# Attention probabilities split into fp16 halves before they are turned, and turned by DMA transposes

## What is computed

```python
def combine_by_denominator(outs, lses):
    w = jax.nn.softmax(jnp.stack(lses, axis=0), axis=0)
    return jnp.einsum('pbth,pbthe->bthe', w, jnp.stack(outs, axis=0))

def dilated_attention_prompt(q, k, v):
    outs, lses = [], []
    for window, dil in DILATIONS:          # (128, 1), (512, 4), (2048, 16)
        o, l = _banded_dilated(q, k, v, window // dil, dil)
        outs.append(o)
        lses.append(l)
    return combine_by_denominator(outs, lses).astype(q.dtype)
```

## Time and profile before

| | us |
|---|---|
| median of 3 runs | 1707.12 |
| lowest and highest run | 1706.36, 1707.31 |
| span of the profiled execution | 1704.6 |
| busy in it: TensorE | 1547.2 |
| VectorE | 847.6 |
| ScalarE | 457.3 |
| GpSimd | 207.6 |

### The profile page before, as it was taken

The page is one execution under the profiler, slowest core; times in us unless marked ns, Lnnn a source line. Parts: engine busy times, 40 slices in busy tenths (PEclk is TensorE's granted clock), DMA queues, the critical chain, the costliest instruction groups (busy, mean ns, idle before and its releaser), DMA issues. The chain is left out here.

```text
span 1704.6 us, 26185 instructions
## 1 busy us (share of the span) xinstructions
PE 1547.2 (91%) x9324; PEld 878.3 (52%) x9324; DVE 847.6 (50%) x1814; ACT 457.3 (27%) x742; POOL 207.6 (12%) x132
## 2 busy tenths in 40 slices
PE   1699999799999987489799899999999999999996
PEld 1355555456565653134344466546664466645652
DVE  6566766436465576566511245413553145512557
ACT  2321221135344451022311144302441034400310
POOL 3310001010101012422100011100110001100125
PEclk9999999798899998689899999999999999999998
DMA  7001101120202025631100422201221022201002
GB/s 217 25 26 51 35 16 38 37 63 3 61 10 59 26 76 154 215 118 49 53 10 1 128 60 79 58 0 37 74 74 37 15 59 74 74 0 38 13 2 103
DMA packets 107311, 96.62 MB, mean 57 GB/s; under 512 B 6407, under 2 KB 91223, under 8 KB 106983
## 3 DMA queue, kind: packets, MB, share of 16 engines
q1 hardware_dynamic: 107247, 95.77, 18.8%
HBM read 85.78 MB, written 10.15 MB: 56 GB/s over the span
## 5 line engine op out<-in xcount | busy, mean ns | idle before, releaser
L1529 PE MATMUL PS<-all_HT,all_WS 128*128 128x344 f16 x3168 | 465.0, 310 | 4.8 <-POOLq L74 4.8
L1529 PEld LDWEIGHTS PS<-all_HT,all_WS 128*128 128x128 f16 x3168 | 310.5, 98 | 159.7 <-issue 6.6
L1539 PE MATMUL PS<-all_WS,ffn_HG 128*128 128x512 f16 (+1 forms) x792 | 237.7, 379 | 3.9 <-POOL ffn_HG L1624 1.9
L442 PE MATMUL PS<-all_WS,all_HT 128*128 (+3 forms) x864 | 194.5, 382 | 3.8 <-POOLq L74 3.8
L1598 ACT ACTIVATE ffn_C<-PS,all_CW,all_CWS 128x1032 f32<-128x1032 f32 x44 | 53.0, 1205 | 379.8 <-PE PS L1529 379.8
L740 PE MATMUL PS<-all_WS,all_HT 128*128 (+3 forms) x864 | 148.4, 329 | 5.5 <-POOLq L74 3.4
L1539 PE MATMUL PS<-ffn_WD,ffn_HG 128*128 128x512 f16 (+1 forms) x396 | 150.1, 379 | 0.0
L1624 POOL TENSOR_TENSOR ffn_HG<-ffn_PRD,ffn_HG 128x1032 f32 (+1 forms) x22 | 47.2, 2146 | 766.4 <-ACT ffn_HG L1610 766.4
L442 PEld LDWEIGHTS PS<-all_WS,all_HT 128*128 128x128 f16 (+1 forms) x864 | 83.7, 97 | 101.4 <-POOLq L74 3.9
L1539 PEld LDWEIGHTS PS<-all_WS,ffn_HG 128*128 (+2 forms) x792 | 76.5, 97 | 101.1 <-issue 8.2
L740 PEld LDWEIGHTS PS<-all_WS,all_HT 128*128 128x128 f16 (+1 forms) x864 | 82.8, 97 | 60.8 <-issue 8.5
(11 more groups left out here) (198 smaller groups left out, 1862.0 us busy)
## 6 DMA issues: line engine op xcount, KB each, us to landing
ffn_SU<-in_w_up SPq DMA_DIRECT2D x42, 512.0 KB, 5.0
ffn_SD<-in_w_down SPq DMA_DIRECT2D x22, 512.0 KB, 3.4
all_STG<-in_w_in SPq DMA_DIRECT2D x32, 256.0 KB, 3.2
all_STG<-in_w_in SPq DMA_DIRECT2D x32, 192.0 KB, 2.7
samples_KC<-in_cache_k_win SPq DMA_DIRECT2D x24, 256.0 KB, 3.8
all_HRES<-in_x_prompt SPq DMA_DIRECT2D x8, 512.0 KB, 5.4
out<-attention_QKV SPq DMA_DIRECT2D x8, 512.0 KB
all_STG<-in_w_out SPq DMA_DIRECT2D x8, 512.0 KB, 3.8
```

The costliest lines, as they stand in the source:

```text
L442: mm = nc.tensor.matmul(Z(s)[:n], HT[:, a, k, s * P:s * P + n], WS[:, slot, b, k, :], start=(k == 0 and (a, b) == (0, 0)), stop=(k == KD - ...
L1529: mm = nc.tensor.matmul(U(x)[:, third], UW[:, u, a, k, x * P:(x + 1) * P], HT[:, b, k, third * T3:(third + 1) * T3], start=(k == 0 and (a, ...
L1539: mm = nc.tensor.matmul(DB[u][:rows, half], HG[:, a, l, ds(t * P, rows)], WD[b][:, l, half * 512:(half + 1) * 512], start=(l == 0 and (a, ...
```

## The change

ScalarE makes the high half straight from PR in SBUF one call after the exp (into the new buffer P16), GpSimd makes the low half as PR minus the high half, and SP issues two DMA transposes for each unit, SBUF to SBUF, that write the turned blocks into PRT. TensorE no longer turns the probabilities, and VectorE no longer makes the low half. PRT now has six slots (even units in PRTL, eight blocks wide; odd ones in PRTS, four wide), and the products of unit n stand five calls behind its scores instead of four (LAG). VectorE's maximum of unit n waits for the low half of unit n - 3. SP's program is written out for the four pairs instead of looped; the transposes of a pair stand behind its output stores and ahead of the next pair's weight loads, and the last two of the eight `w_out` loads stand behind the transposes of units 4 and 8 of the last pair. Each slot of PRT has a semaphore of its own.

```diff
-            PRT = sb(st, "PRT", [P, 3, 2, NT, P], F16)
+            P16 = sb(st, "P16", [P, 3, 2, SEQ], F16)
+            PRTL = sb(st, "PRTL", [P, 3, 2, NT, P], F16)
+            PRTS = sb(st, "PRTS", [P, 3, 2, NT // 2, P], F16)
...
-            PT = (PS[:, 3:5], PS[:, 5:6])
+
+            def PRT(m):
+
+                return (PRTL if m % 2 == 0 else PRTS)[:, m // 2 % 3]
+
+            LAG = 5
...
+            p_turned = sems("p_turned0 p_turned1 p_turned2 p_turned3 p_turned4 p_turned5")
+
+            def turns(p, m):
+
+                used = (NQ + 5 - m % 6) // 6
+                return 32 * used * p + 32 * (m // 6 + 1)
...
                 @block.sync
...
+                        for n in range(NQ):
+                            q = Q_ORDER[n][1]
+                            w = (q + 1) * P
+                            sp.wait_ge(o_ready, BASE + NQ * p + (n - 5 if n >= 6 else (-3, -2, -1, 0, -4, -4)[n]))
+                            for a, ready in ((0, p_hi), (1, p_lo)):
+                                sp.wait_ge(ready, BASE + NQ * p + n + 1)
+                                sp.dma_start_transpose(PRT(n)[:, a, 0:q + 1], P16[:, n % 3, a, 0:w]).then_inc(p_turned[n % 6], 16)
+                            if last and n in (4, 8):
+                                load_out(5 + n // 4)
...
                 @block.gpsimd
...
+                        for n in range(NQ):
+                            w = (Q_ORDER[n][1] + 1) * P
+                            pool.wait_ge(p_hi, BASE + NQ * p + n + 1)
+                            if n >= 3:
+                                pool.wait_ge(p_turned[(n - 3) % 6], BASE + turns(p, n - 3))
...
+                            nc.gpsimd.tensor_tensor(P16[:, n % 3, 1, 0:w], PR[:, n % 3, 0:w], P16[:, n % 3, 0, 0:w],
+                                                    ALU.subtract).then_inc(p_lo, 1)
...
                 @block.tensor
...
-                        m = n - 2
-                        if 0 <= m < NQ:
-                            pe.wait_ge(exp_ready, BASE + NQ * p + m + 1)
...
-                            for kb in range(q + 1):
-                                mm = nc.tensor.transpose(PT[m % 2][:, kb // 4, (kb % 4) * P:(kb % 4 + 1) * P],
-                                                         PR[:, m % 3, kb * P:(kb + 1) * P], IDENT[:])
-                            mm.then_inc(p_turned, 1)
-                        m = n - 4
+                        m = n - LAG
                         if 0 <= m < NQ:
                             h, q = Q_ORDER[m]
-                            pe.wait_ge(prt_low, BASE + NQ * p + m + 1)
+                            pe.wait_ge(p_turned[m % 6], BASE + turns(p, m))
...
                 @block.scalar
...
-                            nc.scalar.activation(PRT[:, m % 3, 0, 0:q + 1],
-                                                 PT[m % 2].rearrange("p b (k n) -> p (b k) n", k=4)[:, 0:q + 1], ACT.Copy).then_inc(prt_ready, 1)
...
+                        m = n - 1
+                        if 0 <= m < NQ:
+                            w = (Q_ORDER[m][1] + 1) * P
+                            act.wait_ge(exp_ready, BASE + NQ * p + m + 1)
+                            if m >= 3:
+                                act.wait_ge(p_turned[(m - 3) % 6], BASE + turns(p, m - 3))
...
+                            nc.scalar.activation(P16[:, m % 3, 0, 0:w], PR[:, m % 3, 0:w], ACT.Copy).then_inc(p_hi, 1)
...
                 @block.vector
...
-                        m = n - 3
-                        if 0 <= m < NQ:
-                            q = Q_ORDER[m][1]
-                            dve.wait_ge(prt_ready, BASE + NQ * p + m + 1)
-                            nc.vector.tensor_tensor(PRT[:, m % 3, 1, 0:q + 1],
-                                                    PT[m % 2].rearrange("p b (k n) -> p (b k) n", k=4)[:, 0:q + 1],
-                                                    PRT[:, m % 3, 0, 0:q + 1], ALU.subtract).then_inc(prt_low, 1)
...
-                            dve.wait_ge(p_turned, BASE + NQ * p + n - 2)
+                            dve.wait_ge(p_lo, BASE + NQ * p + n - 2)
...
-    nc = bacc.Bacc("TRN2", target_bir_lowering=False, num_devices=1)
+    nc = bacc.Bacc("TRN2", target_bir_lowering=False, num_devices=1, dynamic_dma_scratch_size=1024)
```

More of the change, by code:

```diff
@@ L656, in body, with load_out @@
                                              w_in_v[:, 2 * c + k, 4:7, p + 1, :]).then_inc(w_in_s[c % 2], 16)
-                        for k in range(KD if last else 0):
+                        def load_out(k):
                             sp.wait_ge(w_free, BASE + 4 * p + k + 1)
                             sp.dma_start(STG[:, k % 2], w_out[0, k * P:(k + 1) * P].rearrange("p (c n) -> p c n", c=2)).then_inc(w_in_s[k % 2], 16)
+                        for k in range(6 if last else 0):
+                            load_out(k)
                         sp.wait_ge(rotated, BASE + 18 * p + 18)
@@ L668, in body @@
                                      QKV[:NB, NT].rearrange("b (j n) -> b j n", j=3)).then_inc(out_st, 16)
-                    steps(body)(sp)
+                        for n in range(NQ):
[7 more added lines that the diff above has]
+                                load_out(5 + n // 4)
+                    for p in range(HP):
+                        body(sp, p, p == HP - 1)
                     sp.wait_ge(out_st, BASE + 80 * HP)
@@ L683, in body @@
                         nc.gpsimd.tensor_tensor(V16[:, 1], QKV[:, 0:NT, 256:384], V16[:, 0], ALU.subtract).then_inc(v_lo, 1)
+                        for n in range(NQ):
[3 more added lines that the diff above has]
+                                pool.wait_ge(p_turned[(n - 3) % 6], BASE + turns(p, n - 3))
+                            elif not isinstance(p, int) or p > 0:
+                                pool.wait_ge(p_turned[(NQ + n - 3) % 6], BASE + turns(p - 1, NQ + n - 3))
+                            pool.sem_inc(pool_go, 1)
+                            nc.gpsimd.tensor_tensor(P16[:, n % 3, 1, 0:w], PR[:, n % 3, 0:w], P16[:, n % 3, 0, 0:w],
+                                                    ALU.subtract).then_inc(p_lo, 1)
                     steps(body)(pool)
@@ L750, in body @@
                                 mm.then_inc(z_turned, 1)
-                            if kind != "first" and s < 4:
+                            if kind != "first" and s < LAG:
                                 attend(NQ + s, p - 1)
@@ L754, in body @@
                                 pe.wait_ge(att_ready, BASE + NQ * p)
+                                pe.wait_ge(mlo, BASE + p - 1)
                                 for t in range(NT):
@@ L791, in attend @@
                                                  bias=NMX[:, n % 3:n % 3 + 1], accum_out=SUM[:, n % 8:n % 8 + 1]).then_inc(exp_ready, 1)
+                        m = n - 1
[4 more added lines that the diff above has]
+                                act.wait_ge(p_turned[(m - 3) % 6], BASE + turns(p, m - 3))
+                            elif not isinstance(p, int) or p > 0:
+                                act.wait_ge(p_turned[(NQ + m - 3) % 6], BASE + turns(p - 1, NQ + m - 3))
+                            nc.scalar.activation(P16[:, m % 3, 0, 0:w], PR[:, m % 3, 0:w], ACT.Copy).then_inc(p_hi, 1)
                     def body(act, p, kind):
@@ L799, in body @@
                         for s in range(NT + 2):
-                            if kind != "first" and s < 2:
+                            if kind != "first" and s < 1:
                                 attend(NQ + s, p - 1, False)
@@ L860, in attend @@
                                                     ALU.mult, ALU.add).then_inc(neg_ready, 1)
-                        m = n - 5
+                        m = n - LAG - 1
                         if 0 <= m < NQ:
@@ L874, in body @@
                         for s in range(NT + 1):
-                            if kind != "first" and s < 5:
+                            if kind != "first" and s < LAG + 1:
                                 attend(NQ + s, p - 1, False)
```

15 lines of the change are left out of this document (3 added, 12 removed).

## The result

The changed kernel takes **1740.88 us** (median of 4 runs, 1738.58 to 1743.91), the kernel before 1706.91 in the runs beside it: ratio **1.020, 95% interval 1.0183 to 1.0217**. The forecast was 1732 (1710 to 1755), and slower.

What follows compares the result with a forecast made beforehand. Attend phases were bound by TensorE at half clock, then by VectorE; after the change, by half-clock TensorE. Phases +9, projections +12, tail +4 give +25: 1704.6 + 25 + 2.5 = 1732 us, range 1710 to 1755.

Steps and rivals of the forecast that it cites:

- my two readings: DMA moving price of one 128x128 block: 0.22 us taken from packet costs, 0.12 us from the output stores' rate.
- C: Rival for the attend phases: reading and writing each cost a packet, 0.45 us a block, 1822 us in all; chance 0.20.
- D: Rival for the DMA transposes: blocks go one after another at 1.07 us each, about 2140 us in all; chance 0.13.
- Rival A: Attend phases: cheap blocks and issues, clock comes back, ScalarE paces at 28.8 us a phase; 1689 us in all; chance 0.32.
- three times 36.8: Attend phases before the change: the first three taken at 36.8 us each, the last at 33.2.
- my own 38.1: Attend phase after the change: 35.1 us of TensorE work at half clock plus 3 us idle, 38.1 us.
- not the bound: Path through SP's transposes in the attend phase: unit 10 lands at 34.2 us, so TensorE bounds instead.
- A unit comes every 2.14 us: SP's transposes in the attend phase: 32 issues of 1.07 us take 34.2 us a pair.
- 9.0 us after the first score: Start of the attend phase: when the first low half is ready, after exps, copy and GpSimd's subtraction.
- 8 us at half clock lose 4 each: Start of three projections: each begins at half clock for 8 us and loses 4, +12 us together.
- The late weight loads: Next pair's weight loads, queued behind SP's transposes: land 2.7 us after issue, put at no cost.
- some of it in place of TensorE's turn: Tail after the last pair: open chain of copy, subtraction, issue and landing, partly replacing TensorE's turn; +4 us.

Runs made afterwards that it cites:

- e11: e10 plus ten more unused identity turns on TensorE ahead of the first pair's first score; 1692.34 us, 0.993 of the kernel before.
- e12: The kernel before the change, with ten unused identity turns on TensorE ahead of the first pair's first score; 1705.55 us, ratio 0.9994.
- e5: The changed kernel with one matmul pass of three in the attention's scores and products; 1730.3 us, ratio 1.0124.
- e7: e1 with products seven calls behind the scores instead of five and four buffers for the halves instead of three; 1723.84 us, ratio 1.0093.
- e9: e7 with four buffers for the fp32 probabilities, sixteen sums, and the last call's copy ahead of this call's exp; 1715.26 us, ratio 1.0045.
- e1: The changed kernel with both halves of a unit turned by one transpose, 16 issues a pair instead of 32; 1738.98 us, ratio 1.0192.
- e8: e7 with the unused identity turns of e2 on TensorE; 1729.69 us, ratio 1.0128.
- e10: e9 with the unused identity turns of e2 on TensorE; 1704.01 us, ratio 0.9982.
- e4: The changed kernel with the subtraction on VectorE, two calls behind, in place of GpSimd; 1775.57 us, ratio 1.0396.
- e6: e1 with one matmul pass of three in the attention's scores and products; 1712.02 us, ratio 1.0026.
- e2: The changed kernel with as many unused identity turns behind the scores as TensorE lost; 1751.71 us, ratio 1.0271.

## Why the prediction was right, and where not

**Right in sign and on the clock, in part on what holds the phase.** L844 and its 48.0 us are gone from VectorE, whose busy time fell by 36.6 us, and it was worth nothing: TensorE's clock stayed at 0.51 for the whole phase. Its work there is 34.5 us against 35.1 forecast. ScalarE's copy came out at 672 ns (forecast 673). GpSimd's subtraction took 20.8 us a pair (19). The block cost 0.19 us: from 385 to 412 us the transposes made 12779 packets in 69.6% of 16 x 27 us, 23.5 ns each, and a block is 128 of them over 16 engines. That is between my two readings (0.22 taken, 0.12 the low end), and C and D fall. Rival A falls as made, but e11 shows that its full clock can be had in a loosened version with added turns, whose phases of 29.2 to 33.4 us (44 blocks of products) stand against A's 28.8 (55).

The total is nearer than its terms: the phases came out 12.8 us and the tail 4.4 over the forecast, the projections 7.4 under it. That these cancel in part is luck.

**The phases, +21.8 for +9.** Two steps failed. The first is "three times 36.8": the third phase of before takes 33.2 us, and I had carried the first one's row over to it. With the phases as they are (37.4 + 36.6 + 33.2) my own 38.1 would have given +12. Nor is 33.2 a fixed length: the same code takes 35.9 us in the third phase of e12.

The other 9.8 us come from the path through the issues, which I had called "not the bound". I priced an issue at 1.07 us by the scratch store; it costs 1.24. "A unit comes every 2.14 us" and lands, for unit 10, "at 34.2": unit 0 is issued at 380.45 and unit 10 at 408.45, 2.8 us a unit, with waits between. Its second transpose is issued 1.3 us later and with the median landing of 2.7 is there at about 412.5, 39 us after the first score; the phase takes 40.8. I had compared SP with TensorE as if the longer of the two would be the phase, and had put TensorE at half clock first. e5 turns that round: the issues hold a phase of 38.5 us with TensorE 38% busy, and TensorE's other two passes add 2.3. That e7, at 37.9 us, comes near my 38.1 is a coincidence of lengths: its phase has 72 x 0.346 + 44 x 0.186 = 33.1 us of work and some 5 of waits, where my sum had 35.1 and 3, and e9 brings it to 36.5.

Two smaller sums are off and change nothing: the terms of "9.0 us after the first score" add up to 9.3, and C with 0.53 us a block gives about 1858, not 1865.

**The projections, +4.6 for +12.** "8 us at half clock lose 4 each" was too much. The clock was back in under 6 us: 0.65 on average from 414.35 to 420.30, which loses 5.95 x 0.35 = 2.1 us. I had taken the time of the last phase of before, where TensorE waits between scores. The late weight loads cost nothing I can find: TensorE was busy 41.7 of 43.95 us.

**The tail, +8.4 for +4.** I added the new chain once, "some of it in place of TensorE's turn". Behind the last score the products of several units are still open, and each waits for its own transpose and at half clock (TensorE's timeline of the changed kernel):

```profile
672.53 1.14 PE L747 MATMUL PS<-attention_V,attention_PRTL 128*128 128x64 f16 x18 [1.43 <-DMA attention_PRTL<-attention_P]
676.02 0.50 PE L747 MATMUL PS<-attention_V,attention_PRTS 128*128 128x64 f16 x6 [2.35 <-DMA attention_PRTS<-attention_P]
678.58 0.98 PE L747 MATMUL PS<-attention_V,attention_PRTL 128*128 128x64 f16 x15 [2.06 <-DMA attention_PRTL<-attention_P]
680.93 0.34 PE L747 MATMUL PS<-attention_V,attention_PRTS 128*128 128x64 f16 x3 [1.37 <-DMA attention_PRTS<-attention_P]
```

The steps of 2.4 to 3.5 us between them are SP's rhythm again, where each unit's product takes 0.3 to 1.1 us. With half the issues (e1) the tail is 15.1 us in place of 19.4.

**The rule and the rows.** The Trainium skill, VectorE: DVE Perf Modes, section "The three transpose paths", has 1309 ns for one 128x128 block through the DMA. That is of the size of one issue here (1.24 us), but issues of one to eight blocks cost the same and a block in flow costs 0.19 us, so taking 144 blocks one after another by it would be wrong; the traces decide. The Trainium skill, DMA: Bandwidth & Descriptors, section "Latency and other measured facts", has 261 GB/s for transposes with a middle dimension that is not contiguous, an estimated 0.13 us a block, closer than the other and still below the 0.19 measured.

**What stays open.** Why TensorE stayed at half clock through a phase in which it was always busy (e8, e10) is open. In e10 and e11 the second phase has the clock at 0.90 and takes 4 us more than the third; no run says why. e10's executions range from 1702.0 to 1712.4 us and e11's from 1688.1 to 1703.7, mostly with lower mean clocks in the longer ones, so how long the clock stays up isn't fixed. Whether GpSimd's long subtraction cost the changed kernel anything wasn't separated, since e4 brought a wait of its own. Nor was the gain of e7 split between its buffers and its lag.

## What to carry to other kernels

Work taken off TensorE can take its clock with it: here 75 matmuls fewer in the first phase left it busy as long, at 0.51 in place of 0.77. Price the stretch at half clock first, and only then ask which other engine is next. A DMA transpose has a price per instruction on the queue that issues it (1.24 us here), so put as many blocks as the data allow into one, and give the path behind it buffers and lag for the 2.3 to 4.9 us that it took to land here. Where bounds lie as close as 34, 34.5 and 38.5 us, an experiment on one of them can show nothing or a loss; take two away together, as e6 and e7 did, before you call a part harmless.

## What the runs showed that I had not expected

- TensorE was 100% busy for 50.1 us at a granted clock of 0.50 (e10, first phase); with the same instructions and a clock of 1.00 the third phase took 29.2 us. Being busy did not bring the clock back there; in e2, with the same turns, it came back at 400 us.
- The issue of a DMA transpose didn't depend on its width up to eight blocks: medians of 1231 ns (one to four) and 1261 ns (five to eight). With ten to sixteen blocks (e1) it was 1515 ns, against 1234 for two to eight.
- A filler can pay: 288 unused turns and ten more, in the loosened kernel, turned 1715.3 us (e9) into 1692.3 (e11); in the unloosened one the 288 cost 11 us (e2).
